# Another order of loads, norm and first products in the opening of a two-block kernel

## The reference, cut to what matters

```
def _rmsnorm(x, g):
    xf = x.astype(jnp.float32)
    y = xf * lax.rsqrt(jnp.mean(xf * xf, axis=-1, keepdims=True) + EPS)
    return (y * g.astype(jnp.float32)).astype(x.dtype)

def _modulate(h, shift, scale):
    return h * (1 + scale[:, None, :]) + shift[:, None, :]

    c_act = jax.nn.silu(c)
        mod = c_act @ w_ada[l] + b_ada[l]
        sh1, sc1, gt1, sh2, sc2, gt2 = jnp.split(mod, 6, axis=-1)
        h = _modulate(_rmsnorm(x, g_mix[l]), sh1, sc1)
        x = x + gt1[:, None, :] * _mixer(h, w_in[l], ...)
```

## Time and profile before

| | us |
|---|---|
| median of the runs | 1654.88 |
| time of the profiled execution | 1656.27 |
| span of the profiled execution | 1654.5 |
| PE busy | 1631.2 (99%) |
| DVE busy | 1072.2 (65%) |
| ACT busy | 737.4 (45%) |
| GpSimd (POOL) busy | 237.6 (14%) |

### The profile page before, as it was taken

How to read it: one execution, slowest core, us unless ns; L and a number is a source line. 1 busy time by engine, 2 the same in 40 slices (tenths; PEclk the granted TensorE clock), 3 DMA queues, 4 the chain that set the end, 5 groups by cost and what they waited for, 6 DMA issues and landing times.

```text
span 1654.5 us, 20244 instructions
## 1 busy us (share of the span) xinstructions
PE 1631.2 (99%) x7833; PEld 1308.0 (79%) x7833; DVE 1072.2 (65%) x1358; ACT 737.4 (45%) x971; POOL 237.6 (14%) x255
## 2 busy tenths in 40 slices
PE   6999999999999999999999999999999999999999
PEld 3887778888898887887666788886688888888887
DVE  2897778543575577786766855548768876642464
ACT  3543334322374235646775433538822464431242
POOL 0014300050220000001766000004600000000000
PEclk9999999999999999999999999999999999999999
DMA  9556423222222232225664222220032222222223
GB/s 378 197 205 255 161 77 102 89 90 102 103 102 102 88 142 81 103 76 202 211 221 156 77 102 74 100 98 27 2 128 96 83 102 103 99 82 100 102 102 102
DMA packets 31151, 199.30 MB, mean 120 GB/s; under 512 B 3504, under 2 KB 4008, under 8 KB 10832
## 3 DMA queue, kind: packets, MB, share of 16 engines
q1 hardware_dynamic: 27168, 171.63, 28.9%
q10 hardware_dynamic: 3888, 26.38, 4.0%
HBM read 193.60 MB, written 4.40 MB: 120 GB/s over the span
## 4 chain that ended last, share of the span: by engine, by line
PE 90%; DVE 6%; ACT 2%; DMA 1%; issue 1%; POOL 0%; SPq 0%; DVEq 0%; ACTq 0%; POOLq 0%
PE bank1to L1869 14%; PE bank1to L1871 14%; PE bank1to L1870 14%; PE bank L1869 13%; PE bank L1870 12%; PE bank L1871 12%; PE bank L2319 2%; PE bank1to L2435 2%; PE bank L2447 1%; PE bank L2461 1%; DVE w_lo L1016 1%; DMA x<-x_in 1%; DVE ada_sum L1152 1%; PE bank L2153 1%; PE bank L1977 1%
## 5 line engine op out<-in xcount | busy, mean ns | idle before, releaser
L477 ACT ACTIVATE w_hi<-raw 128x2048 fp32r<-128x2048 f32 (+1 forms) x133 | 247.4, 1860 | 312.9 <-DMA raw<-slabs 300.2
L1016 DVE TENSOR_TENSOR w_lo<-raw,w_hi 128x2048 fp32r<-128x2048 f32 (+1 forms) x125 | 291.6, 2333 | 100.3 <-ACT w_hi L477 96.8
L1869 PE MATMUL bank<-h,w_hi 128*128 128x512 f32 (+1 forms) x736 | 290.5, 395 | 0.9 <-ACT qa L477 0.7
L1870 PE MATMUL bank<-h,w_hi 128*128 128x512 f32 (+1 forms) x736 | 285.9, 388 | 0.0
L1871 PE MATMUL bank<-h,w_lo 128*128 128x512 f32 (+1 forms) x736 | 285.6, 388 | 0.0
L1869 PEld LDWEIGHTS bank<-h,w_hi 128*128 128x128 f32 x736 | 138.2, 188 | 35.5 <-issue 7.8
L1871 PEld LDWEIGHTS bank<-h,w_lo 128*128 128x128 f32 x736 | 138.2, 188 | 28.9
L1870 PEld LDWEIGHTS bank<-h,w_hi 128*128 128x128 f32 x736 | 138.3, 188 | 27.9 <-issue 1.0
L1869 PE MATMUL bank1to<-h,w_hi 128*128 128x512 f32 (+1 forms) x416 | 159.7, 384 | 0.0
L1871 PE MATMUL bank1to<-h,w_lo 128*128 128x512 f32 (+1 forms) x416 | 159.3, 383 | 0.0
L1870 PE MATMUL bank1to<-h,w_hi 128*128 128x512 f32 (+1 forms) x416 | 159.3, 383 | 0.0
(11 more groups left out here) (519 smaller groups left out, 2746.1 us busy)
## 6 DMA issues: line engine op xcount, KB each, us to landing
raw<-slabs SPq DMA_DIRECT2D x127, 1024.0 KB, 4.8
ada_chunk<-ada ACTq DMA_DIRECT2D x24, 1024.0 KB, 8.1
p<-sum_rows SPq DMA_DIRECT2D x32, 640.0 KB, 5.5
x<-x_in SPq DMA_DIRECT2D x4, 1024.0 KB, 8.5
p<-decay_rows SPq DMA_DIRECT2D x6, 640.0 KB, 7.4
spill_x<-x SPq DMA_DIRECT2D x1, 2048.0 KB, 10.8
x<-spill_x SPq DMA_DIRECT2D x2, 1024.0 KB, 5.9
out<-x SPq DMA_DIRECT2D x8, 256.0 KB, 2.0
```

Source lines behind the costliest of these rows:

```text
L477: return act.activation(out, in_, f, **kw)
L1016: do.tell(dve.tensor_tensor(w_lo[:, n % SLOTS, part], raw[:, n % SLOTS, part], w_hi[:, n % SLOTS, part].bitcast(f32), ALU.subtract), "w_sp ...
L1869: pe.matmul(out, w[0], a[0], start=start, stop=False)
L1870: pe.matmul(out, w[0], a[1], start=False, stop=False)
```

## The change

Loads. The second half of `x` goes first on ACT's queue instead of second on SP's. Each chunk of `w_ada` now holds two feature tiles of one group, so that chunks 0 to 3 give the scale and chunks 4 to 7 the shift; a row of the copy is two pieces of 4 KB instead of one of 8 KB. `gw` is issued after chunk 3 has landed, slab 1 behind it, and slab 2 after chunk 7.

Norm. DVE adds the eight squares, PE makes token columns of the totals (four matmuls with one column each), ACT and DVE work on 128x4 numbers, and PE spreads the result over the partitions into bank 6 (`spread`). DVE then multiplies all of `x` in place by it.

First product. PE multiplies the queries with the scaled and not yet shifted tiles; the chunks of the shift and its turn stand between the k of that product. The shift's share of the queries comes from 32 matmuls with two columns (`shift_product`), and ACT adds it as a bias when it empties the banks. Then all tiles are made again with the shift; the gates' product alone waits for them, behind the queries. The split of `gw` moves from DVE to GpSimd. ACT's refills of `w_ada` chunks 8 to 11 come later. Elsewhere semaphores are only renamed or shared.

```diff
         def _(sp):
             sp.dma_start(cols[:], cols_d).then_inc(sem("cols_in"), 16)
-            for k in range(0, KT, 4):
-                sp.dma_start(x[:, k:k + 4, :], x_d[:, k:k + 4, :]).then_inc(sem("x_in"), 16)
+            sp.dma_start(x[:, 0:4, :], x_d[:, 0:4, :]).then_inc(sem("x_in"), 16)
             sp.dma_start(consts[:], consts_d).then_inc(sem("consts_in"), 16)
-            sp.dma_start(gw[:], gate_w_d).then_inc(sem("consts_in"), 16)
...
                 if n == 1:
-                    sp.wait_ge(sem("ada_in6"), 16)
+                    sp.wait_ge(sem("ada_in3"), 16)
+                    sp.dma_start(gw[:], gate_w_d).then_inc(sem("gate_w_in"), 16)
+                if n == 2:
+                    sp.wait_ge(sem("ada_in7"), 16)
...
+            act.dma_start(x[:, 4:8, :], x_d[:, 4:8, :]).then_inc(sem("x_in"), 16)
             for n in range(KT):
-                ada_load(n)
+                two, first = 2 * (n % 4), (1 - n // 4) * D
+                act.dma_start(ada_chunk[n][:].rearrange("p (k e) -> p k e", k=2),
+                              ada_d[two:two + 2, :, first:first + D].rearrange("k p e -> p k e")).then_inc(sem(f"ada_in{n}"), 16)
...
-            norm()
+            for k in range(KT):
+                if k >= 4:
+                    act.wait_ge(sem("sq_used"), max(1, k - 4))
+                do.tell(fn(squares_ring[k % 4], x[:, k, :], ACT.Square), "sq_ready", k + 1)
+            act.wait_ge(sem("first_total"), 2)
+            n_root = 1
+            do.tell(fn(first_root, banks[7][:, 0:TOK], ACT.Sqrt, bias=eps), "root_ready", n_root)
             weight_head(0)
...
             mod_copy(0, banks[4])
+            act.wait_ge(sem("h_scaled"), KT)
+            for k in range(KT):
+                do.tell(fn(h_hi[:, k, :], x[:, k, :], ACT.Copy, scale=gain[:, k:k + 1]), "unshifted_head", k + 1)
+            weight_head(1)
+            mod_copy(1, banks[5])
+            act.wait_ge(sem("shift_split"), 1)
+            for k in range(KT):
+                if k < KT - 1:
+                    act.wait_ge(sem("unshifted_used"), k + 1)
+                else:
+                    act.wait_ge(sem("tile_done"), 2)
+                do.tell(fn(h_hi[:, k, :], x[:, k, :], ACT.Identity, scale=gain[:, k:k + 1], bias=mod[:, SH1 + k:SH1 + k + 1]),
+                        "h_head", k + 1)
             ada_refill(KT, KT + 2)
-            heads(1, SH1)
+            weight_head(2)
+            act.wait_ge(sem("shift_taken"), 1)
+            for t in range(2):
+                tile_ready("q_0", t)
+                free(fn(qk[:, t, :], banks[t][:], ACT.Identity, scale=DH ** -0.5, bias=shift_bias[:, t:t + 1]), "q_0", t)
+            act.wait_ge(sem("h_ready"), KT)
             ada_refill(KT + 2, KT + 4)
-            for n in range(1, 3):
-                weight_head(n)
...
         @block.vector
-            dve.wait_ge(sem("consts_in"), 32)
-            do.tell(split(gw_hi[:], gw_lo[:], gw[:]), "gate_w_split", 1)
-            inverse_root(rs)
-            weight_tail(0)
-            mod_third(0)
-            mod_gain(0, SC1, "g_mix")
-            modulated(1, lambda k: gain[:, k:k + 1], SH1)
+            total = rs[:]
+            dve.wait_ge(sem("sq_ready"), 2)
+            do.tell(dve.tensor_tensor(total, squares_ring[0], squares_ring[1], ALU.add), "sq_used", 1)
+            for k in range(2, KT):
+                ...
+            do.tell(dve.reciprocal(first_root, first_root), "first_total", 3)
+            dve.wait_ge(sem("first_total"), 4)
+            for k in range(KT):
+                do(dve.tensor_tensor(x[:, k, :], x[:, k, :], root_bank[:], ALU.mult))
+                if k == 3:
+                    weight_tail(0)
...
+            def shifted(k):
+                do(dve.tensor_scalar((t0, t1)[k % 2][:], x[:, k, :], gain[:, k:k + 1], mod[:, SH1 + k:SH1 + k + 1], ALU.mult, ALU.add))
...
+            dve.wait_ge(sem("shift_done"), 1)
+            do(dve.tensor_reduce(shift_bias[:], banks[7][:, 0:4].rearrange("p (m e) -> p m e", m=2), AX.X, ALU.add))
+            do.tell(dve.tensor_scalar(shift_bias[:], shift_bias[:], DH ** -0.5, None, ALU.mult), "shift_taken", 1)
+            weight_tail(2)
             do(dve.memset(row_parts[:].bitcast(f32), 0.0))
-            for n in range(1, 3):
-                weight_tail(n)
...
         @block.gpsimd
+            pool.wait_ge(sem("gate_w_in"), 16)
+            do(pool.tensor_copy(gw_hi[:], gw[:]))
+            do.tell(pool.tensor_tensor(gw_lo[:], gw[:], gw_hi[:].bitcast(f32), ALU.subtract), "gate_w_split", 1)
```

More of the change, by code:

```diff
@@ L574, in root_copy @@
                 do.tell(fn(rs[:], root_bank[:], ACT.Copy), "root_copied", n)
-            def norm():
-                squares([x[:, k, :] for k in range(KT)], sq)
-                root(rs)
             def heads(stage, shift=None, place=h_hi, between=None):
@@ L980, in _ @@
                         unscaled_head(4, m, u4_hi, col("g_ffn2", m), ("bank_free", FREED["wo"]))
-            root(rs, totals=4)
+            root(totals=4)
             weight_head(SLAB0["upa"] + 2)
@@ new lines, in _, with first_mod @@
+            for k in range(KT):
+                do(dve.tensor_tensor(x[:, k, :], x[:, k, :], root_bank[:], ALU.mult))
+                if k == 3:
+                    weight_tail(0)
+            def first_mod(nth, first, bank):
+                dve.wait_ge(sem("mod_done"), nth + 1)
+                turned = bank[:].rearrange("p (m i r) -> p i m r", m=4, i=4)[:, :, :, 0]
+                place = mod[:, first:first + KT].rearrange("p (i m) -> p i m", i=2)
+                bias = cols[:, COLS["b_ada"] + first:COLS["b_ada"] + first + KT].rearrange("p (i m) -> p i m", i=2)
+                do(dve.tensor_tensor(place, turned[:, 0:2, :], bias, ALU.add))
+                do(dve.tensor_tensor(place, place, turned[:, 2:4, :], ALU.add))
@@ new lines, in _ @@
+            first_mod(0, SC1, banks[4])
+            dve.scalar_tensor_tensor(gain[:, 0:KT], mod[:, SC1:SC1 + KT], 1.0, cols[:, COLS["g_mix"]:COLS["g_mix"] + KT],
+                                     ALU.add, ALU.mult).then_inc(sem("h_scaled"), KT)
+            dve.wait_ge(sem("h_scaled"), KT)
+            for k in range(KT):
+                dve.wait_ge(sem("unshifted_head"), k + 1)
+                do.tell(dve.scalar_tensor_tensor(h_lo[:, k, :], x[:, k, :], gain[:, k:k + 1], h_hi[:, k, :].bitcast(f32),
+                                                 ALU.mult, ALU.subtract), "unshifted_ready", k + 1)
@@ new lines, in _ @@
+            for k in range(KT):
+                if k + 1 < KT:
+                    shifted(k + 1)
+                dve.wait_ge(sem("h_head"), k + 1)
+                do.tell(dve.tensor_tensor(h_lo[:, k, :], (t0, t1)[k % 2][:], h_hi[:, k, :].bitcast(f32), ALU.subtract), "h_ready", k + 1)
+            do.tell(dve.tensor_copy(small[:, 2:3], small[:, 0:1]), "root_used", n_root)
+            dve.wait_ge(sem("shift_done"), 1)
+            do(dve.tensor_reduce(shift_bias[:], banks[7][:, 0:4].rearrange("p (m e) -> p m e", m=2), AX.X, ALU.add))
@@ L1282, in weighted @@
                 if n >= 2:
-                    do.tell(last, "p1_made", n + 1)
+                    do.tell(last, "weighted_made", n + 1)
                     return
@@ L2109, in _ @@
                         last.then_inc(sem("tile_done"), 1)
+                    elif m:
+                        last.then_inc(sem("unshifted_used"), 1)
+                for n in {2: (4, 5), 4: (6,), 5: (7,)}.get(k, ()):
+                    mod_chunk(n)
+                if k == 6:
+                    mod_turn(1, banks[5])
+            for k in range(KT):
+                shift_product(k, SLAB0["q_0"], banks[7], 1)
+            pe.wait_ge(sem("gate_w_split"), 1)
+            for k in range(KT):
+                pe.wait_ge(sem("h_ready"), k + 1)
+                gates = three(banks[5][:], (gw_hi[:, k, :], gw_lo[:, k, :]), (h_hi[:, k, :], h_lo[:, k, :]), k == 0, k == KT - 1)
+            gates.then_inc(sem("gates_done"), 1)
             for t in range(2):
```

218 lines of the change are left out of this document (102 added, 116 removed).

## The result

The changed kernel takes 1668.26 us (median of 4 runs, 1667.65 to 1668.52), the kernel before 1655.04 in the same job: ratio 1.0079, interval 1.0062 to 1.0097. It is slower by some 13 us, where 1.2 were predicted, far outside the range of 1653.6 to 1658.8. The spans of the profiled executions are 1666.7 and 1654.5, 12.2 apart. The keys start at 70.26 instead of 57.55, 12.7 later, and VectorE's long chain begins 12.7 later too (105.16 instead of 92.45). All of the loss is made before the keys.

What follows compares the result with a forecast made beforehand. The opening's path to the first product, then VectorE's long chain from 92.45, was taken to bound the kernel. First product 9.3 earlier, keys 0.6 later, softplus 3.3 later, long chain 1.2 later: 1656.1 us, range 1653.6 to 1658.8.

Steps and rivals of the forecast that it cites:

- likeliest case: Whole kernel: 1.2 us slower, 1656.1 us, own range 1654.8 to 1657.6, chance 0.59.
- The other loads ... All hidden, whatever the shares of the two queues: Opening: chunk 1 lands by 16.4, chunk 3 by 21.3, chunk 7 with gw and slab 1 by 35, all in time.
- Norm, 16.8 to 21.0: Opening: from the total at 16.8, totals 1.1, root and hand-offs, reciprocal 0.2 and spread 1.3 end at 21.0.
- GpSimd's split, 0.4: Before the first product: GpSimd's split of gw delays VectorE by 0.4 us, between 0 and 2.4.
- rival 3: GpSimd's split stands in front of VectorE's gain at full length: +3.2 us, 1658.1; chance 0.08.
- E: Start of the new first product on TensorE: 31.8 us, 9.3 earlier than 41.14.
- E to the keys, 26.3: First product to keys: TensorE waits for VectorE's shifted tiles in the gates; keys start at E + 26.3 = 58.1.
- rival 2: First product: a pause makes TensorE slow, half pace for 5.6 us costing 2.8; +4.0 us, 1658.9; chance 0.12.
- The end: Behind the keys: softplus 3.3 us later, slack of 2.07 hides most, VectorE's long chain starts 1.2 later.
- Rival 1: Opening terms all at their lower end: keys at 56.6, about -1.0 us, 1653.9; chance 0.17.
- signs of being wrong: Keys before 56, product matmuls 0.43 apart, slab 0's w_lo over 3 us, or a new TensorE wait behind 130.
- signs of being right: First product 31 to 32.5, x 10 to 11, gates waiting, keys 57.5 to 59, softplus 61 to 62, later waits changed.

Runs made afterwards that it cites:

- experiment 1: Kernel after, with the first eight chunks of w_ada laid out as one 8 KB piece per row: 1663.15 us, ratio 1.0050.
- 2: Kernel after, rows of 4 KB kept, chunks 4 to 7 issued by SyncE once chunk 2 has landed: 1661.06 us, ratio 1.0038.
- 3: Kernel before, with its first eight chunks in two 4 KB pieces a row: 1656.92 us, ratio 1.0008.
- experiment 7: Kernel after, with GpSimd's split of the gate weights waiting for the gain: 1667.19 us, ratio 1.0072.
- experiment 5: Kernel after with only two of the 32 two-column products of the shift: 1667.74 us, ratio 1.0070.
- 6: Experiment 2 with 32 instead of 14 fillers before the first product: 1661.47 us, ratio 1.0038 to the kernel before.
- experiment 10: Experiment 9, with only x, columns and constants queued until x lands, second slab's split behind shifted tiles, shift turned behind the third: 1655.68 us, ratio 1.0000.
- 14: Kernel before with x first, 8 KB rows, norm on token columns with all fillers, gates and query still together: 1653.60 us, ratio 0.9985.
- 9: Experiment 8 with the shift product turned round, 16 products of 256 moving weight columns instead of 32 two-column ones: 1657.77 us, ratio 1.0011.
- 11: Experiment 10 with columns first, gate weights behind all chunks, two chunk sums in the product, softplus ahead of the slab: 1656.15 us, ratio 1.0007.
- experiment 8: Kernel after, all chunks issued by SyncE, chunks 4 to 6 summed before the first product, shift turned behind the fourth tile: 1658.41 us, ratio 1.0020.

## Why the prediction was wrong

The sign of its likeliest case was right, and so was the idea that the second half of the change gives back what the first half gains; the size was off by 12. The failed step made 5.8 of it, TensorE's clock 2.9; the rest are terms that I had too small.

- **Failed step: "The other loads ... All hidden, whatever the shares of the two queues".** I worked out when each load lands and never what its issue costs the engine that issues it, though I counted two refills on the same queue at 0.8. ScalarE was held from 4.55 to 13.89, and the squares began at 16.2 instead of 10.4: 5.8 us. Experiments 1 and 2 started the squares 4.9 and 5.7 sooner and gave 5.1 and 7.2 of the time back (a part of it GpSimd's, below); 3 showed the same hold-up without the change. The landing of x itself was right (10.3 against 10.4). The profile of the kernel after shows the hold-up as issue time; the Trainium skill ("Perfetto Trace Analysis", DMA Instruction — HWDGE) says that the reported instruction lasts until its descriptors are made, and speaks of more descriptors than the buffer holds. The trace agrees as far as it can: twice the pieces a row, 13.4 us instead of 4.4. That a full buffer is the reason is not shown.
- **Norm, 16.8 to 21.0.** The total took 6.45 us behind the squares' start (predicted 6.4). From there to the scaling I had 4.2, measured 6.1: totals 1.86 for 1.1, spread 2.04 for 1.3. I had named "up to twice that" of 0.89 and then took near the lower end. It was the upper end in every version with this norm: 1.86 or 1.87.
- **GpSimd's split, 0.4.** Measured 1.0 (experiment 7). The mechanism was right. It fell beside the low part since that stood 7.8 us later and gw only 3.3. In experiment 1 it fell beside the gain, as rival 3 had it, and that took 0.93 instead of 0.17.
- **E.** Predicted 31.8, measured 40.4: 5.8 + 1.9 + 0.6 (1.0 less the 0.4 counted) and a rest of 0.3. With the issues mended it was 33.7.
- **E to the keys, 26.3.** Measured 29.9. The parts that VectorE sets came as worked out: shifted tiles 0.55 and 0.69, 10.45 us from the first to the last (10.4). Of the 3.6 too much, 2.9 is the clock. It fell at the first product, behind the 2.79 us wait: 1.6, by the traces in which it did not fall (experiments 5 and 6: 14.20 us from E to the turn in both). That is rival 2, whose condition was met because VectorE came late; it had a price of 2.8. And it fell in the small products of the shift, so that the keys followed the last low part by 2.14 instead of 0.8: 1.3. This second fall was in no rival. I had priced these products at 0.11 each and had not asked what they do to the clock. The last 0.7 is the product itself: it took 14.2 us to the turn at full clock, where I had counted 13.5.
- **The end.** I let 3.3 us of delay at the softplus, more than at the keys, shrink to 1.2 in a slack of 2.07. Measured, the softplus came 14.3 late (72.60) and the keys 12.7. VectorE's wait ahead of its long chain went from 2.07 to 0.54 and was not gone. So the slack hid the softplus's extra delay whole, the keys set the 12.7, and the span took 12.2.

As a sum for the keys: 58.1 predicted, + 8.6 (E) + 3.6 (E to keys) = 70.3. Rival 1 (all at the lower end) had it the wrong way round: no term ended there. Of the signs of being wrong two showed, matmuls 0.43 apart and a low part of slab 0 over 3 us; of the signs of being right only the landing of x did. TensorE did not wait in the gates, since it was slow itself, and the product that had waited 1.59 us at 129.86 waits 1.53, not over 2.

What the change could have brought at best stays partly open. With its faults mended (10) it stands level with the kernel before. It adds the shift product (1.9 us in its better form) and two splits of every tile instead of one (8 low parts of 0.75 on VectorE), and in experiment 10 TensorE waits 0.82 and 1.50 us for two chunks ahead of its first product. The front half alone (14) is the faster kernel.

## What to carry to other kernels

Ask of each load not only when it lands, but how long its issue holds the engine that issues it, and what work of that engine it now stands in front of; a queue of loads with narrow rows belongs on an engine with nothing else to do. When a chain is divided so that its first half can start sooner, add up what each later engine then does twice before counting the gain. Products with very few moving columns are not cheap on TensorE: turn them round, so that the wide operand moves.

## What the runs showed of the hardware

- Eight issues of 1 MB from ScalarE take 4.4 to 4.7 us with rows of 8 KB and 13.0 to 13.6 with rows in two pieces of 4 KB, in both kernels; in the kernel after the first five are not slow (0.67 on average), the next two take 9.3 together.
- Behind 32 two-column matmuls, 0.11 us apart, the granted clock fell to 0.50 in all six traces that have them in a row, and with four of them between every three wide ones it stayed at 0.50 for 16 us with TensorE never idle (one trace; another execution of the four did not show it in its time). It stayed at 1.00 behind sixteen products of 256 moving columns, 0.114 us apart (experiments 9 to 11), and through gates with waits in between (experiment 5).
- With x first in both queues, holding the chunks back did not bring it sooner: it landed at 9.0 with chunks, constants and gate weights behind it on SyncE's queue (experiment 8), and at 9.1 with the chunks held back (10). With the columns ahead of one half it was otherwise: 9.9 with the chunks held back (11), 10.5 with chunks of 4 KB rows behind it on ScalarE's queue (2), 11.3 with rows of 8 KB (1). The columns, 227 KB behind a half of x in one queue, landed 2 us (8) and 1.2 us (10) after that half.
